# Output products of a hybrid decoder trunk spread between narrow compressed scores, and the second tile's first products moved in front of the compressed transposes

## What is computed

```python
proj = x @ w_in[i]
conv_out = b_g * _causal_dwconv(c_g * h, short_conv_w[i])
...
sc = jnp.einsum('bgrqd,bgcd->bgrqc', qc, k_cmp)          # 15 compressed keys per kv group
p_cmp = _masked_softmax(sc, cmp_end[None, :] <= t[:, None])
o_cmp = jnp.einsum('bgrqc,bgcd->bgrqd', p_cmp, v_cmp)
...
out = g[..., 0:1] * unchunk(o_c) + g[..., 1:2] * unchunk(o_s) + g[..., 2:3] * unchunk(o_w)
mixed = _head_rmsnorm(jnp.concatenate([conv_out, attn_out], -1), head_norm_g[i])
x = _layer_norm(ALPHA * x + mixed @ w_out[i], ln1_g[i], ln1_b[i])
```

## Time and profile before

| | |
|---|---|
| runs | 708.83, 710.58, 712.25 us; median 710.58 |
| profiled execution | 709.42 us, of which the span is 707.6 |
| PE busy | 98% of the span |
| DVE, ACT, POOL busy | 70%, 49%, 22% |
| mean granted clock of TensorE | 0.985 |

### The profile page before, as it was taken

One profiled execution on the slowest core, in us unless ns is written; L12 is line 12 of the kernel. 1 busy time (PEld: TensorE's weight loads), 2 busy tenths in 40 slices (PEclk: granted clock), 3 DMA queues, 4 the chain that ended last, 5 costly groups with the idle time before them and its releaser, 6 DMA issues.

```text
span 707.6 us, 11957 instructions
## 1 busy us (share of the span) xinstructions
PE 690.6 (98%) x4822; PEld 631.8 (89%) x4822; DVE 492.1 (70%) x698; ACT 345.1 (49%) x492; POOL 158.6 (22%) x54
## 2 busy tenths in 40 slices
PE   8999999999999999999999999999999999999995
PEld 5899999888999999999778999988889999999994
DVE  4675768877996666666786457686869766666646
ACT  5654535414865444444347444453258555555520
POOL 0000020230174444440000000113106444444300
PEclk9999999899999999999999999997999999999998
DMA  9972443333875555556248143432357755555301
GB/s 290 323 249 62 142 156 119 120 119 106 282 241 195 191 195 196 194 188 179 78 148 269 61 150 118 152 102 78 119 200 245 269 179 179 179 178 178 119 0 60
DMA packets 87403, 116.85 MB, mean 165 GB/s; under 512 B 5230, under 2 KB 73536, under 8 KB 87360
## 3 DMA queue, kind: packets, MB, share of 16 engines
q1 hardware_dynamic: 85920, 111.85, 47.3%
q10 hardware_dynamic: 1440, 4.39, 1.8%
HBM read 115.19 MB, written 1.05 MB: 164 GB/s over the span
## 4 chain that ended last, share of the span: by engine, by line
PE 92%; DVE 5%; DMA 1%; issue 1%; ACT 1%; SPq 0%; DVEq 0%; ACTq 0%
PE bank L1154 28%; PE bank L1155 27%; PE bank L1156 27%; PE bank L1239 3%; PE bank L1226 2%; DMA x_tok<-in_x 1%; PE bank L1175 1%; DVE x_tok L941 1%; DVE stats L925 1%; DVE x_tok L923 1%; PE bank L1218 1%; DVE ring_lo L290 1%; DVE x_tok L949 1%; PE bank L1328 1%; PE bank L1305 0%
## 5 line engine op out<-in xcount | busy, mean ns | idle before, releaser
L290 DVE TENSOR_TENSOR ring_lo<-raw,ring_hi 128x2048 fp32r<-128x2048 f32 x102 | 232.5, 2284 | 21.6 <-ACT ring_hi L286 21.5
L1154 PE MATMUL bank<-xh,ring_hi 128*128 128x256 f32 x832 | 237.6, 286 | 0.0
L1156 PE MATMUL bank<-xh,ring_lo 128*128 128x256 f32 x832 | 235.8, 283 | 0.0
L1155 PE MATMUL bank<-xl,ring_hi 128*128 128x256 f32 x832 | 235.7, 283 | 0.0
L286 ACT ACTIVATE ring_hi<-raw 128x2048 fp32r<-128x2048 f32 x102 | 194.4, 1909 | 11.9 <-DMA raw<-in_w_in 9.1
L693 POOL COPY step_par<-ffn_par 128x16 f32 (+1 forms) x22 | 127.5, 5800 | 170.9 <-DVE work L962 170.9
L1154 PEld LDWEIGHTS bank<-xh,ring_hi 128*128 128x128 f32 x832 | 159.8, 192 | 0.9
L1155 PEld LDWEIGHTS bank<-xl,ring_hi 128*128 128x128 f32 x832 | 159.8, 192 | 0.6
L1156 PEld LDWEIGHTS bank<-xh,ring_lo 128*128 128x128 f32 x832 | 159.7, 192 | 0.0
L962 DVE SCALAR_TENSOR_TENSOR work<-bank,step_par,work 128x255 f32<-128x255 f32 (+1 forms) x176 | 72.2, 474 | 95.2 <-ACT work L532 95.1
L532 ACT ACTIVATE work<-bank,step_par 128x256 f32<-128x256 f32 x88 | 44.2, 560 | 117.1 <-PE bank L1156 117.1
(11 more groups left out here) (178 smaller groups left out, 785.6 us busy)
## 6 DMA issues: line engine op xcount, KB each, us to landing
raw<-in_w_up SPq DMA_DIRECT2D x44, 1024.0 KB, 5.2
raw<-in_w_down SPq DMA_DIRECT2D x22, 1024.0 KB, 5.3
raw<-in_w_in SPq DMA_DIRECT2D x21, 1024.0 KB, 5.2
raw<-in_cmp_w SPq DMA_DIRECT2D x8, 1024.0 KB, 5.9
raw<-in_w_out SPq DMA_DIRECT2D x8, 1024.0 KB, 4.9
qkv<-in_ln_g ACTq DMA_DIRECT2D x4, 512.0 KB, 3.4
qkv<-in_ln_b ACTq DMA_DIRECT2D x4, 512.0 KB, 4.9
raw<-in_w_in SPq DMA_DIRECT2D x2, 512.0 KB, 5.6
```

The costliest lines, as they stand in the source:

```text
L290: eng.tensor_tensor(ring_lo[slot_of(L, u)][:], raw[raw_of(L, u)][:], ring_hi[slot_of(L, u)][:].bitcast(fp32), ALU.subtract).then_inc(split ...
L1154: pe.matmul(dst, ah, bh, start=start, stop=False, **kw)
L1155: pe.matmul(dst, ah, bl, start=False, stop=False, **kw)
L1156: return pe.matmul(dst, al, bh, start=False, stop=stop, **kw)
```

## The change

`cmp_scores` now takes the four output products of blocks 0 and 1 for tile 0 (twelve wide matmuls) between its narrow ones: one output product after every second compressed score. So the two products in front of `mean_squares` and the two in front of `transpose_cmp` are gone from there, and the semaphore of the scores (`s_done`) is signalled by the last narrow matmul, ahead of the last wide three. The four output products of blocks 0 and 1 for tile 1 move from behind `times_v_cmp` to in front of `transpose_cmp`; they write banks 0 and 1, and wait for the exponentials of unit 11 and for `max_done` of the compressed scores, where before they waited for the compressed exponentials.

```diff
@@ cmp_scores
                         ins = mm3(bank[0][:, c0:c0 + NG * NBLK], qTh[:, h, tok], qTl[:, h, tok],
                                   *(a[:].rearrange("p g c -> p (g c)") for a in (kcTh, kcTl)), True, True)
-                ins.then_inc(s_done, 1)
+                        if h == NPAIR - 1 and t == TT - 1:
+                            ins.then_inc(s_done, 1)
+                        if h % 2:
+                            wait_mix(L, 0, t)
+                            out_product(L, 0, h // 2, t)
@@ the loop over n
                     elif n == 10:
                         pe.wait_ge(conv_out, 2 * L + 2)
-                        out_part(L, 0, 0, 0)
+                        wait_unit(L, U_OUT)
                         mean_squares(L, 1)
                         cmp_scores(L)
@@ behind the loop
-                out_part(L, 0, 0, 1)
+                pe.wait_ge(exp_done, N_ATT * L + 12)
+                pe.wait_ge(max_done, N_ATT * L + 13)
+                out_part(L, 1, 0, 0)
+                out_part(L, 1, 0, 1)
                 transpose_cmp(L)
                 conv_roots(L, 1)
                 times_v_cmp(L, 0)
                 times_v_cmp(L, 1)
-                pe.wait_ge(exp_done, N_ATT * L + 13)
-                out_part(L, 1, 0, 0)
-                out_part(L, 1, 0, 1)
                 out_unit(L, 0, 1)
```

## The result

| | median | lowest to highest | runs |
|---|---|---|---|
| before | 711.41 us | 708.83 to 713.85 | 6 |
| changed | 724.17 us | 721.85 to 726.10 | 6 |

The ratio is 1.0191, with a 95% interval of 1.0161 to 1.0220 (the medians alone give 1.018). The prediction was 711.8 us, with a range of 707.5 to 716. In the tables further down, runs more than 1.5% above the fastest of their kernel are left out of the ratio, though not of the median and the range: one of before's (717.19), two of `first_ahead`'s, three of `fill_ahead`'s and one of `first_fill`'s. The profiled execution of the changed kernel took 721.85 us, 12.4 more than the 709.42 of before.

The account below looks back on a forecast made before the run. The prediction took PE as the bound, slowed by its clock, with the DVE and POOL chain hidden 0.3 us below it. Clock held gives 709.2 us; one fall at 2.6 makes 711.8, range 707.5 to 716.

Parts of the forecast that it names:

- steps 1 to 5: Layer 0 from the mixed block to the second `heads_T`, clock held: ends 0.1 us later; layer 1 ends 1.5 earlier.
- The hole: Before blocks 2 and 3 in each layer: PE waits 1.8 us for `xl` from DVE.
- The small waits: PE waits 0.35 us before tile 1's products, 0.6 before `times_v_cmp` and 0.5 before the second `heads_T`.
- the price of one fall: One clock fall around the mixed block costs 2.6 us, taken between 1.7 and 3.4.
- one fall in one of two layers: Main forecast, 38%: DVE chain takes PE's gain and the clock falls once, 709.2 + 2.6 = 711.8 us.
- the quiet run ahead: Short matmuls before the first wide one at 127.0, 1.5 us or 3.5 with what precedes, may make the clock fall.
- The rival by the page: Only an idle engine makes the clock fall, so spreading gapless work changes nothing; named within the 4% case at 717.7 us.
- 4% on 717.7: Clock falls whatever stands between; slow stretches of 6.8 and 10.2 us stay: 709.2 + 3.4 + 5.1, chance 4%.
- the six cases: Whole-kernel times: 711.8 us (38%), 709.2 (24%), 714.4 (22%), 717.7 (4%), 707.4 or 705.6 (9%), 702 (3%).
- the 22% case: Clock falls in both layers from the quiet run before the first wide matmul: 709.2 + 5.2 = 714.4 us, chance 22%.

Follow-up runs that it names:

- first_ahead: Changed kernel with one of the block's four tile 0 output products put ahead of the mean squares; median 708.85 us, ratio 1.0011.
- fill_ahead: Changed kernel plus twelve unused matmuls a layer, six ahead of the mean squares and six behind; median 711.63 us, ratio 1.0017.
- first_fill: Changed kernel with one tile 0 product ahead of the mean squares, tile 1's block 1 behind `times_v_cmp`, six unused matmuls a layer around the mean squares; 714.40 us.
- move_only: Kernel before with only tile 1's products moved in front of the compressed transposes; median 715.38 us, ratio 1.0116.
- before_early5: Kernel before with six unused matmuls a layer in PE's idle 0.64 us ahead of unit 10's transposes, twelve runs; median 708.81 us, ratio 0.9976.
- before_again: Kernel before profiled once more without any edit; 713.93 us.
- fill_block: Changed kernel with 24 unused matmuls a layer, six after each six narrow matmuls and none ahead of the block; 729.69 us in one run.

## Why the prediction was wrong

**Right: steps 1 to 5, the sum if the clock holds.** The chain from the transposes to the heads, hidden 0.3 us below PE's pace, does take PE's gain. The hole was given at 1.8 and measured 1.86 in both layers. With the clock held I had 708.0 for the profiled execution; `first_ahead`, the same work with one product earlier, has five of ten runs at 707.6 to 708.0. The small waits were over-read (0.20 for 0.35, 0.6 and 0.5), and PE's own pieces took that much longer.

**Wrong: the price and the number of falls.** The step that failed reads "so I take 2.6 as the price of one fall, between 1.7 (half of 3.4) and 3.4", with a forecast of one fall in one of two layers. The two profiles of the changed kernel have slow stretches of 13.4 + 3.1 and 16.8 us, and of 16.9 + 3.2 and 13.4 + 3.2: 16.5 to 20 us a layer and about 8 to 10 us lost in each, less what runs beside the waits, and in both layers of both profiles. On the time: 721.85 less the 708.0 of the sum is 13.9 us for two layers, 6.9 each, where one fall at 2.6 was forecast. My argument for a short stretch, "Wide matmuls come earlier now than in either, and in layer 0 the slow stretch ended about 2 us behind the first of them", does not hold. In layer 0 of the old order the clock came back within a run of six wide matmuls, just ahead of the last (137.16). In the new order groups of six narrow and three wide, at half clock, passed by up to four times without its coming back. It came back within tile 1's twelve wide ones in three of the four layers profiled, and in layer 1 of the first profile 0.7 us ahead of them. Layer 1 of the old order spoke against the argument from the start: its slow stretch up to 485.10 holds all six of its wide matmuls (480.85 to 483.56) and 1.5 us more.

```profile
480.85 0.78 PE L1154 MATMUL bank<-ring_hi,xh 128*128 128x512 f32 x1
...
483.56 0.63 PE L1296 MATMUL bank<-cst,probs 128*120 128x128 f32 x2
```

The longest stretch seen before (10.1) was no bound for an order that had not been run.

**Half right: the quiet run ahead.** The fall in layer 0 came at about 128.1, 1.4 us behind the start of the first wide matmul (126.75) and within the block. `first_ahead` and `fill_ahead` show that this run decides it. But the fall at 124 to 124.2 comes before it, in both kernels, and I did not have it: the one profile of before had a fall there in neither layer; the spread of the run times was a sign, and I did not ask about it.

**A second fall, not foreseen.** Behind the hole of 1.86 the clock fell again: 148.70 to 151.80 in the changed kernel, 145.20 to 148.40 in `move_only`, 144.40 to 147.60 in `first_ahead`. It is 3.1 to 3.2 us long each time, and the prediction put the cost of the hole to the clock at nothing without saying why. It is not certain either: layer 1 of the changed kernel's first profile and both layers of `fill_ahead` have the hole and no such fall.

**The rival by the page.** The Trainium skill, "TensorE: Matmul & The Clock Gate", Part 1, names an idle engine as what lets the clock fall. The second fall and the one at 124 come in or behind idle time (1.86 and 0.64 us). The fall at 130.2 and at 128.1 came with PE gapless for several us, and in `fill_ahead`'s profile the latter is gone with PE gapless in both; short matmuls can cost the clock as idle time does. I had 4% on 717.7 for slow stretches that stay; it was the nearest of the six cases in time and still too low, but its mechanism, that mixing doesn't matter, is not what the runs show. The mechanism of the 22% case, falls in both layers by the quiet run ahead, is what happened in three of the four layers profiled; in the fourth, layer 1 of the first profile, the clock fell at the transposes, over 2 us earlier in the order than the place that I gave (near 127). It cost far more than its 5.2 us.

**Still open.** What brings the clock back. The theory set up after the result, that the order decides mostly how soon the clock returns, is not shown: `first_ahead` mended the time by falling more rarely. In `before_early5` it was slow for 3.2 us (132.1 to 135.3), in the profile of before for 6.7, in `before_again` for 20.3 in spite of six wide matmuls at 126.4 to 128.7; and why `fill_block`'s block won it back in one layer and not in the other is not settled either. The runs say which orders lose it often; how long each keeps it lost rests on one or two profiles of each. The 733.48 of `fill_ahead` and 726.66 of `first_fill` were not profiled.

## What to carry to other kernels

Where the profile shows a clock that falls, ask of a new order first what will stand in front of its first wide matmul: three wide ones put back ahead of the short run took 724 us to 709 here. Ask also how the clock comes back, not only whether it stays up; that long runs of wide matmuls kept whole bring it back sooner is not shown, since six of them did not in layer 1 of the old order or in `before_again`. The longest slow stretch seen so far is a lower bound for one in an order that was never run, and not an upper one. Profile a kernel whose clock moves more than once. And fillers in idle time that is there anyway are a cheap test of whether a clock is the cause: six matmuls in 0.64 us of idle time took off the times above 711 here, and the fastest stayed where they were.

A wait that is filled is not a wait saved when the work behind it hangs on another engine's chain: with the clock held, halving the 1.86 us hole moved the wait to two places upstream.

## What the runs showed of the hardware

- The granted clock fell with PE gapless: behind eight matmuls of 2 columns and, at 0.112 us each, some 22 of 30 columns in layer 0 and 16 in layer 1, and inside a block with a third of its matmuls 512 wide.
- From run to run of one program the fall moves and its length changes: in the kernel before at 130.2 for 6.7 us or at 123.8 for 20.3 in layer 0, at 475.0 for 10.1 or at 482.2 for 6.6 in layer 1 (which runs 6.1 us later there). Times of the kernel before spread from 706.43 us (mean clock 0.993) to 717.19 (0.973) with it.
- A matmul of 2 and one of 30 columns both cost 0.112 us at full clock and 0.21 at half (480.31 to 480.52 and 480.74 in layer 1 of the changed kernel, below): short matmuls pay for the clock like wide ones.

```profile
480.31 0.37 PE L1154 MATMUL bank<-kcTh,qTh 128*128 128x30 f32 x1
480.52 0.37 PE L1155 MATMUL bank<-kcTl,qTh 128*128 128x30 f32 x1
480.74 0.37 PE L1156 MATMUL bank<-kcTh,qTl 128*128 128x30 f32 x1
```
